# The RWKV recurrence of a two-block network, on 64x64 products with the next tile's preparation among the chains

## The reference, cut to what matters

```python
def rwkv7_scan(r, w, k, v, a, b, s0):
    def step(s, inp):
        r_t, w_t, k_t, v_t, a_t, b_t = inp
        sa = jnp.einsum('...vk,...k->...v', s, a_t)
        s = s * w_t[..., None, :] + sa[..., :, None] * b_t[..., None, :] + v_t[..., :, None] * k_t[..., None, :]
        return s, jnp.einsum('...vk,...k->...v', s, r_t)
...
    w_log = -jax.nn.softplus(-(w0 + jnp.einsum('bldr,drc->bldc', jnp.tanh(w_lo), w2))) - 0.5
    decay = jnp.exp(-jnp.exp(w_log.astype(jnp.float32))).astype(cols.dtype)
    iclr = jax.nn.sigmoid(a0 + jnp.einsum('bldr,drc->bldc', a_lo, a2))
    kk = l2norm(heads(k * k_k))
    k_dir = heads(k[:, :, None, :] * (1 + (iclr - 1) * k_a))
    b_dir = kk[:, :, None] * heads(iclr)
    y, s_fin = rwkv7_scan(both_dirs(r_h), per_dir(heads(decay)), per_dir(k_dir), both_dirs(v_h),
                          both_dirs(-kk), per_dir(b_dir), s0)
```

## Time and profile before

| What | Value |
|---|---|
| Median of 2 runs | 3846.27 us (3845.51 to 3847.02) |
| Span of the profiled execution | 3844.3 us; what lies around it is the rest of a run's time, 1.2 us to the lower of the two runs and 2.7 us to the higher |
| Instructions | 36834 |
| TensorE products busy | 3212.1 us, 84% of the span |
| VectorE busy | 1341.1 us, 35% |
| ScalarE busy | 529.4 us, 14% |
| GpSimd busy | 21.2 us, 1% |
| Read from HBM | 305.78 MB, 80 GB/s over the span |

### The profile page before, as it was taken

One profiled execution on the slowest core, in us unless ns is written; L12 is line 12 of the kernel. 1 busy time (PEld: TensorE's weight loads), 2 busy tenths in 40 slices (PEclk: granted clock), 3 DMA queues, 4 the chain that ended last, 5 costly groups with the idle time before them and its releaser, 6 DMA issues. The chain is left out here.

```text
span 3844.3 us, 36834 instructions
## 1 busy us (share of the span) xinstructions
PE 3212.1 (84%) x14306; PEld 2312.6 (60%) x14306; DVE 1341.1 (35%) x3692; ACT 529.4 (14%) x1287; POOL 21.2 (1%) x18
## 2 busy tenths in 40 slices
PE   5978899895989949596969696748887879999998
PEld 2466585364668424485868583337765357777775
DVE  0055231016423012465655564367775120000001
ACT  1023120002312010212121210112211010000000
POOL 0000000010000000000000000000000000000000
PEclk9966999996799979586767687857787969999999
DMA  4321333332134331000000001100000214444432
GB/s 163 141 111 44 131 153 121 142 143 110 55 121 154 142 116 71 17 1 1 1 1 1 1 1 53 66 0 1 1 1 6 106 66 153 153 153 153 152 151 80
DMA packets 25595, 311.29 MB, mean 81 GB/s; under 512 B 2634, under 2 KB 5074, under 8 KB 6738
## 3 DMA queue, kind: packets, MB, share of 16 engines
q1 hardware_dynamic: 25426, 308.95, 21.1%
HBM read 305.78 MB, written 3.16 MB: 80 GB/s over the span
## 5 line engine op out<-in xcount | busy, mean ns | idle before, releaser
L429 PE MATMUL bank<-weight_ring,arena 128*128 128x512 f32 (+5 forms) x1616 | 654.0, 566 | 41.6 <-DVE arena L976 14.6
L429 PEld LDWEIGHTS bank<-weight_ring,arena 128*128 128x128 f32 x1616 | 307.1, 197 | 384.5 <-issue 358.6
L1910 PE MATMUL bank<-arena,weight_ring 128*128 128x256 f32 x2048 | 447.5, 381 | 1.0 <-ACT arena L315 1.0
L1910 PEld LDWEIGHTS bank<-arena,weight_ring 128*128 128x128 f32 x2048 | 391.0, 191 | 61.7 <-issue 7.2
L864 PE MATMUL bank<-arena,weight_ring 128*128 128x256 f32 x1408 | 304.4, 379 | 2.1 <-issue 1.1
L864 PEld LDWEIGHTS bank<-arena,weight_ring 128*128 128x128 f32 x1408 | 267.4, 190 | 39.1 <-issue 1.5
L382 PE MATMUL bank<-constants,arena 128*128 128x128 f32 (+1 forms) x452 | 88.1, 380 | 216.9 <-DVE arena L365 76.3
L1930 DVE TENSOR_TENSOR arena<-bank,arena 128x512 f32<-128x512 f32 x32 | 22.1, 692 | 609.2 <-PE bank L1910 609.2
L1944 PE MATMUL bank<-weight_ring,arena 128*128 128x512 f32 x512 | 222.3, 592 | 0.0
L382 PEld LDWEIGHTS bank<-constants,arena 128*128 128x128 f32 (+1 forms) x452 | 81.3, 202 | 228.7 <-issue 226.0
L317 DVE COPY arena<-bank 128x512 f32<-128x512 f32 (+4 forms) x51 | 32.8, 644 | 452.4 <-PE bank L429 403.5
(11 more groups left out here) (375 smaller groups left out, 3727.6 us busy)
## 6 DMA issues: line engine op xcount, KB each, us to landing
weight_ring<-stream SPq DMA_DIRECT2D x133, 2048.0 KB, 7.3
weight_ring<-stream SPq DMA_DIRECT2D x4, 1024.0 KB, 4.8
arena<-rows_in SPq DMA_DIRECT2D x1, 3264.0 KB
weight_ring<-stream SPq DMA_DIRECT2D x2, 1152.0 KB, 5.2
arena<-constants SPq DMA_DIRECT2D x1, 2200.0 KB
arena<-bias_rows SPq DMA_DIRECT2D x2, 1024.0 KB
arena<-rows_in SPq DMA_DIRECT2D x2, 1024.0 KB
u_rest<-arena SPq DMA_DIRECT2D x1, 2048.0 KB, 6.3
```

Of the source, the lines that this page charges most:

```text
L429: last = nc.tensor.matmul(bank[b][:, 0:nn], left(k, m), w[:, k * n + h0:k * n + h0 + nn], start=(j == 0), stop=(j == kt - 1))
L1910: last = mm(bank[b][:, t * S:(t + 1) * S], w[:, ((2 * j + t) * KD + k) * P:((2 * j + t) * KD + k + 1) * P], tT[:, k, :], start=(k == 0), s ...
```

## The change

The recurrence is written anew. `chain_unit(n, d)` takes the tile of step `n` in direction `d` with all eight heads, and keeps only the 64x64 blocks: a product works on one chunk or one head half, with 64 contraction rows, 64 output partitions and 64 columns, and consecutive products change the half. Constants for it are 64 columns wide (`K2A`), loaded first; the rest (`K2`), which the gated delta branch uses, is loaded behind the recurrence. The two directions run side by side, each with two PSUM banks (`pair[d]`); the other four banks belong to `prep_unit(n, d)`, which prepares the tile of step `n`. `together` takes one round of both chains of step `n`, then one round of both preparations of step `n + 1`. Operands that the chains read are doubled by the parity of `n` or freed by marks (`step_end`, `keys_used`, `prepared`). Waits are written one by one (`pe_after`, `dve_after`, `act_after`, `pool_after`, of one form; one is shown). The inverse norms of the keys of all four tiles come once, in `key_sums`, ahead of everything; two products for the normed keys and two for the bonus go to GpSimd. The decay's factor moves into the exponentials' scale. r is scaled and turned in the latent sequence alone.

The diff is shown less 12 columns of indentation.

```diff
+K2A = offsets([("shift", P), ("shift_n", P), ("shift_p", P), ("eye", CH)]
+  + [(f"{n}{d}", w) for d in range(2) for n, w in (
+      ("cum", P), ("cumx", P), ("col3", 3), ("strictT", CH), ("nstrictT", CH), ("inclT", CH),
+      ("off0", CH), ("off0T", CH), ("lv1", CH), ("lv2", CH), ("lv3", CH), ("lv4", CH), ("lv5", CH))])
+K2 = offsets([("index", 8), ("ones", P), ("reset16", T2 * P), ("reset4", T2 * P // 16)]
...
-        bank = [ctx.enter_context(nc.psum_tensor(f"bank{i}", [P, 512], F32)) for i in range(8)]
+        pair = [ctx.enter_context(nc.psum_tensor(f"pair{i}", [P, 2, 512], F32)) for i in range(4)]
+        bank = [pair[i // 2][:, i % 2, :] for i in range(8)]
...
-kc2 = get(K2["all"])
+kc2 = get(max(K2["all"], K2A["all"]))
...
-load(kc2, k2)
+load(kc2[:, 0:K2A["all"]], k2[:, 0:K2A["all"]])
...
+key_room = chainmem[0].rearrange("p a h n -> p a (h n)")
+def key_sums():
+    sq = key_room.rearrange("p a (h n) -> p (a h) n", n=CH)
+    link(tt(key_room, bc[:, :, 512:1024], row("k_k").unsqueeze(1).to_broadcast([P, T2, 512]), ALU.mult))
+    link(tt(sq, sq, sq, ALU.mult))
+    link(nc.vector.tensor_reduce(rsk.rearrange("p a h -> p (a h)"), sq, AX, ALU.add))
+    return nc.vector.tensor_scalar(rsk, rsk, 1.0, EPS, ALU.mult, ALU.add)
+dve_step(key_sums)
+act_step(lambda: nc.scalar.activation(rsk, rsk, ACT_F.Sqrt))
+dve_step(lambda: nc.vector.reciprocal(rsk, rsk))
+for eng in (PE, DVE, ACT, POOL):
+    if eng:
+        settle(eng)
...
+def dve_after(fn, *marks):
+    if DVE:
+        for who, n in marks:
+            DVE.wait_ge(done[who], n)
+        fn().then_inc(dve_done, 1)
+    c.dve += 1
+    return "dve", c.dve
...
+half = [slice(0, CH), slice(CH, P)]
+QUADS = ((0, 0), (1, 1), (0, 1), (1, 0))
+by8 = lambda a: a.unsqueeze(1).to_broadcast([P, RH, CH])
+eye = k2a("eye", CH)
+exp_scale = math.exp(-0.5)
+keys_used, step_end, prepared, y_mark = {}, {}, {}, {}
...
+def chain_unit(n, d):
+    seq, step = divmod(n, 2)
+    par, late = n % 2, seq == 1
+    T = 2 * seq + (step if d == 0 else 1 - step)
+    pr = pair[d]
+    by_head = pr.rearrange("p g (i w n) -> p (g i) w n", i=4, w=2)
+    by_chunk = pr.rearrange("p c (i w n) -> p c i w n", i=4, w=2)
+    full = [pr[:, b, :].rearrange("p (h n) -> p h n", n=CH) for b in range(2)]
+    X, Xt, Mt, Y, N0, Wt, U = Xs[d], Xts[d], Mts[d], Ys[d], N0s[d], Wts[d], Us[d]
+    rb, rk, av, st, ak = rbs[d], rks[d], avs[d], states[d], Ys[d]
+    aT, rT, bT, kT = aTs[par][d], rTs[par][d], bTs[d], kTs[d]
+    dcol = dcols[par][d]
+    v, bb, kd, aa = [heads(a) for a in (bc[:, T, 1024:1536], bbs[par][d], kds[par][d], aas[par][d])]
+    head_of = lambda q: 2 * (q % 4) + q // 4
+    mask = lambda name: by8(k2a(f"{name}{d}", CH))
...
+    def by_position(w, A, B):
         for i in range(4):
-            last = f(bk[:, n * i:n * i + n], i)
+            for g, c_ in QUADS:
+                last = mm(by_head[half[c_], 4 * g + i, w, :], A[half[g], i, half[c_]], B[half[g], i, half[c_]],
+                          start=True, stop=True)
         return last
-    return fn
+    def in_chunk(o, A, B):
+        for q in range(RH):
+            for c_ in range(2):
+                last = mm(o[half[c_], q, :], A[half[c_], q, :], B[half[c_], q, :], start=True, stop=True)
+        return last
+    def key_products():
+        last = by_position(0, kT, aT)
+        return by_position(1, kT, rT) if late else last
+    p = pe_after(key_products, *ready, *before)
+    def key_masks():
+        last = tt(ak, by_head[:, :, 0, :], mask("strictT"), ALU.mult)
+        return tt(rk, by_head[:, :, 1, :], mask("inclT"), ALU.mult) if late else last
+    m_keys = dve_after(key_masks, p)
+    yield
+    def turned_products():
+        last = by_position(0, bT, aT)
+        return by_position(1, bT, rT) if late else last
+    p = pe_after(turned_products, m_keys)
+    def turned_masks():
+        tt(Mt, by_head[:, :, 0, :], mask("nstrictT"), ALU.mult)
+        link(tt(Xt, by_head[:, :, 0, :], mask("off0T"), ALU.mult))
+        if late:
+            tt(rb, by_head[:, :, 1, :], mask("inclT"), ALU.mult)
+        both = chainmem[d][:, 1:3, :, :].rearrange("p a h n -> p (a h) n")
+        return tt(both, both, eye.unsqueeze(1).to_broadcast([P, 2 * RH, CH]), ALU.add)
+    m_turned = dve_after(turned_masks, p)
+    yield
+    p = pe_after(lambda: by_position(0, aT, bT), m_turned)
+    keys_used[n, d] = p
+    def plain_mask():
+        link(tt(X, by_head[:, :, 0, :], mask("off0"), ALU.mult))
+        return tt(X, X, by8(eye), ALU.add)
+    m_x = dve_after(plain_mask, p)
...
+    def key_values():
+        for q in range(RH):
+            h = head_of(q)
+            for c_ in range(2):
+                last = mm(full[1][half[c_], h, :], ak[half[c_], q, :], v[half[c_], h, :], start=True, stop=True)
+        return last
+    p_av = pe_after(key_values, m_x)
+    m_av = act_after(lambda: copy_act(av, full[1]), p_av)
+    m_xt = m_av
+    for level in range(1, LEVELS):
+        p = pe_after(lambda: in_chunk(full[0], Mt, X), m_x)
+        m_y = dve_after(lambda: tt(Y, full[0], by8(k2a(f"lv{level}{d}", CH)), ALU.mult), p)
+        yield
+        if level < LEVELS - 1:
+            p = pe_after(lambda: in_chunk(full[0], Xt, Y), m_y, m_xt)
+            m_x = act_after(lambda: copy_act(X, full[0]), p)
+        p = pe_after(lambda: in_chunk(full[1], Y, Xt), m_y, m_xt)
+        m_xt = act_after(lambda: copy_act(Xt, full[1]), p)
+        yield
+    m_n0 = dve_after(lambda: tt(N0[:, first, :, :], st, dcol[:, :, 0:1].to_broadcast([P, 4, CH]), ALU.mult), p)
+    def keys_turned():
+        for i in range(4):
+            for c_, g in QUADS:
+                q = 4 * g + i
+                last = mm(by_chunk[half[g], c_, i, 0, :], aa[half[c_], head_of(q), :], Xt[half[c_], q, :],
...
+    yield
+    moved = pr[:, 1, :].rearrange("p (w i n) -> p w i n", w=2, i=4)[:, 0, :, :]
+    def state_values(c_):
+        for i in range(4):
+            for g in range(2):
+                h = 2 * i + g
+                last = mm(moved[half[g], i, :], kd[half[c_], h, :], v[half[c_], h, :], start=(i == 0), stop=False)
+        return last
+    def values():
+        for q in range(RH):
+            for c_ in range(2):
+                mm(full[0][half[c_], q, :], Xt[half[c_], q, :], av[half[c_], head_of(q), :],
+                   start=(q == 0), stop=False)
...
+    yield
+    for c_ in (first, 1 - first):
+        hc = half[c_]
+        def correct(g):
+            for i in range(4):
+                last = mm(full[0][hc, 4 * g + i, :], Wt[half[g], c_, i, :], N0[half[g], c_, i, :],
+                          start=False, stop=(g == 1 and i == 3))
+            return last
+        p = pe_after(lambda: correct(0), p, m_n0)
+        yield
+        p = pe_after(lambda: correct(1), p)
+        m_u = dve_after(lambda: nc.vector.tensor_copy(U[hc, :, :], full[0][hc, :, :]), p)
+        yield
+        def move():
+            if c_ != first:
+                state_values(c_)
+            for i in range(4):
+                for g in range(2):
+                    last = mm(moved[half[g], i, :], bb[hc, 2 * i + g, :], U[hc, 4 * g + i, :],
+                              start=False, stop=(i == 3))
+            return last
+        p = pe_after(move, m_u)
+        def update():
+            link(tt(st, moved, N0[:, c_, :, :], ALU.add))
+            if c_ == first:
+                return tt(N0[:, 1 - c_, :, :], st, dcol[:, :, 1:2].to_broadcast([P, 4, CH]), ALU.mult)
+            return tt(st, st, dcol[:, :, 2:3].to_broadcast([P, 4, CH]), ALU.mult)
+        m_n0 = dve_after(update, p)
+        yield
+    step_end[n, d] = (p, m_n0)
+    if late:
+        def outputs():
+            for i in range(4):
+                for g in range(2):
+                    q = 4 * g + i
+                    for c_ in range(2):
+                        mm(by_head[half[c_], q, 0, :], rb[half[c_], q, :], U[half[c_], q, :],
+                           start=(i == 0), stop=False)
...
+            return last
+        p = pe_after(outputs, m_n0)
+        yield
...
+        o = by_head[:, :, 0, :].rearrange("p (g i) n -> p g i n", g=2)
+        if step == 0:
+            y_mark[T] = dve_after(lambda: nc.vector.tensor_copy(yv, o), p)
+        else:
+            y_mark[T] = dve_after(lambda: tt(yv, yv, o, ALU.add), p, y_mark[T])
+        step_end[n, d] = (p, y_mark[T])
+    yield
+prep_end = {}
...
+def prep_unit(n, d):
+    seq, step = divmod(n, 2)
+    par, late = n % 2, seq == 1
+    T = 2 * seq + (step if d == 0 else 1 - step)
+    b0, b1 = bank[4 + 2 * d], bank[5 + 2 * d]
+    lw, ic, kk = lws[d], ics[d], kks[d]
+    bb, kd, aa, dcol = bbs[par][d], kds[par][d], aas[par][d], dcols[par][d]
+    r, k = bc[:, T, 0:512], bc[:, T, 512:1024]
+    lo = half[d]
+    room, free = prep_end.get(d, ()), step_end.get((n - 2, d), ())
+    def low_rank():
+        mm(b0[:, :], loT[lo, T, 0, :], lora_sb[lo, 0, :], start=True, stop=True)
```

(103 more changed lines are left out.)

351 lines of the change are left out of this document (111 added, 240 removed).

## The result

The changed kernel takes 3412.02 us (median of two runs, 3411.15 to 3412.88) against 3846.27: a ratio of 0.887 [0.885, 0.890], 434 us less. Run again beside other kernels it took 3411.82 (four runs, 3407.84 to 3415.73). The forecast of 3534 us was 122 us too slow, and the range 3420 to 3690 missed the result by 8 us. That rival gave the four tiles 295 us at full clock; they took 302.6 with three tenths of their time at 1.2 GHz, so that its number came out is luck.

A forecast was written before the change was run, and what follows sets the result against it. Bounds: four preparations with TensorE mostly waiting, and chains keeping it busy with half-zero products. Recurrence 464 + 30 + 10 = 504, less 49 for clock, 455 us; 3846.3 - 766.7 + 455 - 1 = 3534 us, range 3420 to 3690.

The forecast's parts named there:

- That rival: Whole recurrence: full clock nearly throughout, recurrence 335 us, kernel 3414 us; chance 0.08.
- Which clock: Recurrence chains: clock rises behind all-row passes; low at tile starts, in state steps and in the last tile.
- the forecast's 415 us: Four tiles of the recurrence: forecast time with the clock up in over half the levels of the first three.
- The price of products in four corners: 64x64 chain products: taken as 0.029 us a pass at full clock and 0.054 at low, two at a time.
- the sum at low clock: Recurrence: four tiles 464 us, first preparation 30, key_sums 10, together 504; waits 5 us a tile early, 7 late.
- the sum at full clock: Recurrence: four tiles 295 us with 12 us of waits in a tile, 40 before them, together 335.
- the bank rival: Chain products writing both halves of one PSUM bank don't pair: 3800 us, or about 3700 at forecast's clock; chance 0.09.
- the rule that it named: VectorE operations with two SBUF inputs and GpSimd operations reading SBUF block each other fully; up to 27 us longer.
- What would show it: Signs in the recurrence: stretch near 455 us, clock up in levels of tiles one to three, down in tile four.
- One pass at a time: Chains: alternating tile positions make each pass wait, 0.107 us each; 3917 us, 4100 with exposed weight loads; chance 0.07.
- Low clock throughout: Whole recurrence at low clock, 504 us, kernel 3583 us; chance 0.25.
- A preparation that isn't hidden: Preparations among the chains: each unit blocks a queue as before, 4 x 43 us, about 3634 us; chance 0.03.

## Why the prediction was wrong

- **The step that failed is "Which clock".** It said that the clock rises behind products over all 128 rows and that a tile without a preparation stays low, 107 us. That tile took 65.4 us. The clock rose in the last tile behind 64x64 products alone, and in every tile's levels with the preparations taken out. I had read one rise, next to L1340 and L1341, as its cause, and 13 us of L1189 and L1277, position products and state outputs, as the rule for all 64x64 products. The levels are other work than those, and they raise it. Nor does alternation hold the clock, nor do two directions. In the state steps it fell even where fillers left TensorE hardly a pause, and only full-row fillers of 256 columns prevented it. Why the state steps lower the clock and the levels don't stays open: the kind of work and its amount were not varied apart.
- **Its size.** The mean clock of the four tiles was 0.848 (the rows above, weighted by their lengths), so 0.30 of their time was at 1.2 GHz. With s the share of the time at low clock, the two sums give the time T by T x (s/464 + (1 - s)/295) = 1; the forecast's 415 us stands for s = 0.79. With s = 0.30 it is 331 us: 84 of the 119 us by which the recurrence was over-estimated (455 against 335.5).
- **The price of products in four corners.** I had 0.029 us a pass for all, from pairs in two corners. L1186 takes 15 ns, L1256 and L1330 are of its form, 1408 passes in all. Together these were busy for 32.0 us, where 0.029 gives 41 and 0.054 gives 76: 9 to 44 us less, according to the clock. That is enough for the other 28 us of the tiles. The waits explain little: TensorE stood idle for 45.7 us in the four tiles, between the 24 of the sum at low clock and the 48 or more of the sum at full clock.
- **The first preparation** took 23.5 us, not 30. `key_sums` took 9.4 for 10.
- **Right:** the count of passes; 0.029 for pairs at full clock (938 records in 27.5 us) and 0.054 at low (32 of L1193 from 1835.11 to 1836.82); pairing inside one bank, 29 ns a pass, against the bank rival and against the wording of the Trainium skill, "TensorEngine Tiling (Array Packing)", Gotcha 1 (the two row halves write different partitions of the bank here; the measurement decides); VectorE at 159 us, no bound over the stretch, against the 180 expected; waits of TensorE at the first rounds because of `turned_masks`, though 20 us over four tiles in place of 3 a tile; and the loads, 6.5 us for the reload against 6.2.
- **GpSimd.** The prediction cost it at nothing, with 27 us as the bound by the rule that it named. It was busy for 29.9 us, the blocking is there, and it holds VectorE up for 4 us.
- **What would show it** was right in its sign: a tile's low clock in its last part was there, but the levels of tile four, said to be down, stood at 1.00 for 28 us. That one line decides between the forecast and its rival.
- **The rivals.** One pass at a time is refuted by 32 ns for a pass against its threshold of 96. Low clock throughout is refuted by the same rows as the forecast. A preparation that isn't hidden, at its old 43 us, is refuted by the time; at its new price most of it isn't hidden either, since taking it out of the chains' rounds costs 13 us only, for three preparations, of which tile three's costs 20. The sum had that right: it counted TensorE's time for them in full.

Where the 434 us come from: over the stretch TensorE's busy time fell from 617.8 us to 274.4, by 343 us, and its idle time from 148.9 to 61.1, by 88. Two groups of the kernel before, its position products:

```profile
L1189 PE MATMUL bank<-arena 64*128 64x128 f32 x512 | 106.4, 405 | 41.8 <-issue 37.7 <-DVE arena L403 4.1
L1207 PE MATMUL bank<-arena 64*128 64x128 f32 x128 | 39.0, 458 | 0.0
```

- **Position products**: up to 145 us of TensorE before (records of the two can overlap), 24.1 now. That is some 120 us, of which the turns of the corners are some 5 by the time measured, not clear of the noise; the fewer and shorter passes and the higher clock were not undone one by one.
- **Levels**: one level of both directions took twice 5.36 us, 10.7, at full clock. It is 192 passes now, 8.6 us at the 45 ns of the run without alternation and 5.6 at 29. So at full clock the smaller products give 2.1 us a level and the alternation 3.0, that is 39 and 57 us over the 4 times 4 2/3 levels. The alternation measured 72 us in all, since it also shortens the passes at low clock. L1193 is busy for 114.0 us, against 200 for the old levels had they all run at full clock, so the levels gave at least 86 us.
- **The preparations among the chains** gave 13.
- **The two directions side by side** are worth 135, but they aren't new cover: four streams stood side by side before.

The rest, four preparations of 43.2 us, each alone, that became one of 23.5 and three like tile three's 20, the solving, the masks and the state steps, was not undone one by one, and how it divides stays open.

## What to carry to other kernels

Price the clock from the kernel's own rows of the same kind of work, and look for the rise where nothing else is beside it: one rise next to a full-row product is no cause. Small products should go to different corners of the array one after the other, and two independent chains should share the queue, since the second covers the masks and copies of the first. A wait that is shown on the busiest engine is not yet time to win: taking 7 us of it away won nothing that could be measured, while loads with nothing to wait for, issued 25 us earlier, gave 9. And a mean over a group can hide two kinds of operation: look at the single ones before you call something a slowdown.

## What the runs showed of the hardware

- 64x64 fp32 passes of 64 columns at full clock: 45 ns each in a run down one chunk, 29 with the chunks by turns, also when both write one PSUM bank, and 15 with four corners in turn, in either order tried.
- The clock rose behind 64x64 products alone (from 0.50 in 1834 to 1838 us to 0.97 in the next 4), and stayed at 2.4 GHz through levels in which TensorE paused 0.8 us after every 3.0.
- It fell in the first rounds, where TensorE stood idle, and in the state steps, also where fillers of 128 columns kept TensorE busy for 5.88 of 6 us ahead of the fall. Fillers of 256 columns over all rows prevented that.
- VectorE beside GpSimd, 128x512: 1.64 and 1.75 us instead of 0.69 where both inputs lie in SBUF, ending 0.55 us behind GpSimd's operation; no change where one input lies in PSUM.
